# Keeping the residual transposed on chip, and streaming 256 tokens past stationary weights, in a two-layer f32 trunk

## The chip, the cores and the metric

The kernel runs on one core of one Trainium2 chip. The time is the device time of one execution in microseconds (us). Of each kernel the median of several executions is taken; one further execution is profiled, and all rows of a trace come from that one.

## The reference

The program is the trunk of a small decoder: 256 tokens (two tiles of 128), model width 1024, two layers, everything in float32. Each layer is: half a SwiGLU FFN, a token mixer, half a SwiGLU FFN, each behind an RMS norm of its own. The first mixer is native sparse attention (NSA), the second is FoX, attention with a forget gate over keys and values that one shared projection of x (here "kv") made. Cut to what matters:

```python
def rms_norm(x, g):
    return x * lax.rsqrt(jnp.mean(x * x, axis=-1, keepdims=True) + EPS) * g
def swiglu(h, w_in, w_out):                     # w_in (1024, 2*2816), w_out (2816, 1024)
    a, b = jnp.split(h @ w_in, 2, axis=-1)
    return (jax.nn.silu(a) * b) @ w_out
for l in range(2):
    if l == 1: k_sh, v_sh, c_sh = shared_kv(x, kv_norm_g, fox_w_kvf, fox_b_f)
    x = x + 0.5 * swiglu(rms_norm(x, norm_g[l, 0]), ffn_w_in[l, 0], ffn_w_out[l, 0])
    h = rms_norm(x, norm_g[l, 1])
    x = x + (nsa_mixer(h, ...) if l == 0 else fox_mixer(h, ...))   # each ends in o @ w_out, (1024, 1024)
    x = x + 0.5 * swiglu(rms_norm(x, norm_g[l, 2]), ffn_w_in[l, 1], ffn_w_out[l, 1])
return rms_norm(x, final_g)
```

## The kernel before

**Precision.** TensorE multiplies f32r, a rounded f32. Every large product is made in three: each operand is split into a high part and a low part (`thi`, `tlo` of the transposed x; `whi`, `wlo` of the weights; `ghi`, `glo` of the hidden tile), and `three` issues high*high, high*low and low*high into one PSUM bank (lines 396 to 398). ScalarE makes high parts (`hi`, lines 858 and 864), VectorE (DVE) low parts (`lo`, lines 1214 and 1220).

**Weights.** They stream from HBM in 166 units of 1 MB, 128 x 2048 f32 each, through a ring of three buffers, in the order in which TensorE wants them. SyncE asks for unit u as soon as the low part of unit u-3 is made; ScalarE overwrites a slot of `whi` when TensorE has used the unit that was in it (semaphore `unit_used`).

**An FFN.** The hidden width 2816 is cut into 11 chunks of 256 columns (of a and of b). A round of the loop (`ffn`) makes the in-product of one chunk (two units, 48 matmuls) and the out-product of the chunk before (one unit, 24 matmuls). The stationary operand is a 128 x 128 piece of tokens, 512 columns of weights stream past it, and the hidden chunk comes out with tokens on the partitions: `inb[t]` holds 256 columns of a and 256 of b of token tile t. ScalarE applies Silu with the row's 1/rms as its scale (`rstd`, one number a partition), VectorE multiplies by b, TensorE turns the result with four transposes (`hidden_turn`, line 487) so that it can be stationary in the out-product, and the two engines split it. The out-product adds up in the four banks `acc` over all 11 chunks; since the order of the writes differs, four bf16 matmuls with zeros open the banks first (line 501).

**Between stages.** The residual is `xs`, with tokens on partitions. At the end of a stage VectorE adds the banks to it one token tile at a time (`ffn_add`, `mixer_add`), ScalarE sums the squares of a row in one instruction, and TensorE turns x (`turn`, line 390), eight transposes a token tile, which `thi` and `tlo` are then split from with the norm's gain. The turning of tile 0 and of tile 1 stands among matmuls of the stage that ends and of the one that begins.

**Rest.** GpSimd (POOL) builds the bias tables for NSA in the first 45 us, through 16 transfers of its own, splits one unit a mixer, and adds attention outputs. There is no scheduler: the order on each engine is the order of the code, and semaphores hold the engines to each other.

Of the kernel before, what the change touches and what calls it, by code (L numbers as in the profile page):

```python
# [21 lines left out]
F32 = mybir.dt.float32  # L22
# [51 lines left out]
NORMS = ["ffn0", "nsa", "ffn1", "kv", "fox", "ffn3", "final"]  # L74
ADDS = ["ffn0", "nsa", "ffn1", "ffn2", "fox", "ffn3"]

TILE0 = ["nsa", "kv", "fox"]
ADD_BEFORE = {"nsa": "ffn0", "ffn1": "nsa", "kv": "ffn1", "fox": "ffn2", "ffn3": "fox", "final": "ffn3"}


def added(name, t, half):

    before = ADD_BEFORE[name]
    return 4 * ADDS.index(before) + (2 * t + half if before.startswith("ffn") else 2 * half + t) + 1
# [16 lines left out]
def yoco_trunk(nc, x, norm_g, ffn_w_in, ffn_w_out, nsa_w_in, nsa_cmp_pos, nsa_cmp_w1, nsa_cmp_w2,  # L101
               nsa_w_out, rel_bias, kv_norm_g, fox_w_kvf, fox_b_f, fox_w_q, fox_w_out, final_g, out):
    ctx = ExitStack()
    with ctx:
# [13 lines left out]
        xs = sb("xs", [P, NT, D])  # L118
# [5 lines left out]
        sa = sb("sa", [P, NT, FC])  # L124
        gg = sb("gg", [P, NT, FC])
# [20 lines left out]
        zeros = sb("zeros", [32, P], BF16)  # L146
# [16 lines left out]
        rstd_h = sb("rstd_h", [P, NT, H])  # L163
# [36 lines left out]
        squares_out = work[:, D:2 * D]  # L200
        fexp = work[0:H, 0:SEQ]
# [25 lines left out]
        s_sumsq = sem("sumsq")  # L227
        s_rms = sem("rms")
        s_rstd = sem("rstd_ready")
        s_rstd_h = sem("rstd_by_head")  # L230
        s_tt = sem("turned")
        s_thi = sem("turned_hi")
        s_tlo = sem("turned_lo")
        s_silu = sem("silu_done")
        s_g = sem("hidden_ready")
        s_gt = sem("hidden_turned")
        s_ghi = sem("hidden_hi")
        s_glo = sem("hidden_lo")
        s_in0 = sem("hidden_cols_tile0")
        s_out_bank = sem("ffn_out_bank")  # L240
        s_tile0 = sem("tile0_done")
# [68 lines left out]
        def _(sp):  # L310
# [20 lines left out]
            def ffn(f):  # L331
                b = U_FFN[f]
                for i in range(2):
                    load(b + i, ffn_in(f, 0, i, b + i))
                    if b + i == 0:
                        sp.dma_start(xs[:, 1, :], x[0, P:2 * P, :]).then_inc(s_x[1], 16)
# [9 lines left out]
            def matrix(w, b, chunks):  # L346

                for c, col in enumerate(chunks):
                    for i in range(2):
                        u = b + 2 * c + i  # L350
# [4 lines left out]
            sp.dma_start(xs[:, 0, :], x[0, 0:P, :]).then_inc(s_x[0], 16)  # L355
# [9 lines left out]
            matrix(nsa_w_out[0], U_NSA_OUT, [0, CW])  # L365
# [4 lines left out]
            matrix(fox_w_out[0], U_FOX_OUT, [0, CW])  # L370
            ffn(3)
            for t in range(NT):
                for n, done in enumerate([s_y, s_ya]):
                    cols = slice(n * CW, (n + 1) * CW)
                    sp.wait_ge(done, t + 1)
                    sp.dma_start(out[0, t * P:(t + 1) * P, cols], xn[:, t, cols]).then_inc(s_out, 16)
# [4 lines left out]
        def _(pe):  # L381
            def turn(name, t):

                for e in range(2):
                    if name == "ffn0":
                        pe.wait_ge(s_x[t], 16)
                    elif name != "ffn2":
                        pe.wait_ge(s_xadd, added(name, t, e))
                    for k in range(4):
                        mm = pe.transpose(tbanks[2 * t + e][:, k * P:(k + 1) * P],  # L390
                                          xs[:, t, (4 * e + k) * P:(4 * e + k + 1) * P], ident[:, :])
                    mm.then_inc(s_tt, 1)

# [6 lines left out]
            def rows4(slot, half, t, o, wait_third=None):  # L400

                tok = slice(t * P, (t + 1) * P)
                for k in range(4):
                    if k == 2 and wait_third:
                        pe.wait_ge(*wait_third)
                    kk = 4 * half + k
                    mm = three(o, thi[:, kk, tok], tlo[:, kk, tok], whi[slot][:, k * CW:(k + 1) * CW],
                               wlo[slot][:, k * CW:(k + 1) * CW], kk == 0, kk == KT - 1)
# [1368 lines left out]
```

## Time and profile before

| | |
|---|---|
| median of 3 runs | 1088.58 us (1088.22 to 1090.03) |
| profiled execution | 1091.58 us, of which the trace spans 1089.8 us |
| granted TensorE clock, mean | 0.988 |
| busy: TensorE, its weight loads | 97%, 80% |
| busy: VectorE, ScalarE, GpSimd | 56%, 48%, 8% |
| matmuls | 5067 |
| read from HBM | 180 MB, 167 GB/s over the span |

The page says which engine was busy for how long. A matmul's record is longer than the distance to the next one's start, since matmuls are pipelined; times of single matmuls are therefore read as distances between starts in the timeline.

### The profile page before, as it was taken

To read this page: it belongs to the slowest core of one execution; us is meant where nothing else is said; L and a number is where in the kernel's file an instruction comes from. 1 tells how busy PE (TensorE), PEld (TensorE's weight loads), DVE (VectorE), ACT (ScalarE), POOL (GpSimd) and SP (SyncE) were. 2 spreads that over 40 slices of the span, in tenths; PEclk is the share of its full clock that TensorE was granted. 3 is DMA by queue.
4 is the path that set the end of the run, shared out by engine and by line. 5 is a ranking of instruction groups with operands and counts; after the bars stand their busy time and mean duration, and the time that the engine had idled before them with its cause. 6 is when DMAs were issued, how large, how long until landed. Compare 5 with 4: busy or idle time off the path is not lost.

```text
span 1089.8 us, 14059 instructions
## 1 busy us (share of the span) xinstructions
PE 1060.1 (97%) x5067; PEld 872.4 (80%) x5067; DVE 612.5 (56%) x844; ACT 522.7 (48%) x751; POOL 89.4 (8%) x112
## 2 busy tenths in 40 slices
PE   8799999999899999999999999999998999999997
PEld 6688888888677888888888878888886788888886
DVE  4444545677767464445556775454557656444454
ACT  7334344666446364443356454444355646444434
POOL 6300000000202100000000192000002000000000
PEclk9899999999889999999999999999999999999999
DMA  9765465456500245555554655555545135555541
GB/s 269 216 208 187 159 231 193 155 176 210 193 1 1 64 163 194 187 191 170 196 185 155 231 194 192 175 191 186 181 155 194 38 97 193 192 182 189 190 171 39
DMA packets 128675, 182.40 MB, mean 167 GB/s; under 512 B 5929, under 2 KB 100241, under 8 KB 128513
## 3 DMA queue, kind: packets, MB, share of 16 engines
q1 hardware_dynamic: 127008, 176.18, 49.0%
q0 software_dynamic: 1456, 5.72, 2.0%
q8 instruction: 21, 0.34, 0.1%
q14 instruction: 14, 0.11, 0.0%
q10 hardware_dynamic: 176, 0.05, 0.0%
HBM read 180.34 MB, written 1.59 MB: 167 GB/s over the span
## 4 chain that ended last, share of the span: by engine, by line
PE 91%; DVE 4%; ACT 2%; DMA 2%; issue 1%; SPq 0%; DVEq 0%; ACTq 0%
PE inb L396 16%; PE inb L398 16%; PE inb L397 16%; PE acc L396 11%; PE acc L398 11%; PE acc L397 11%; DMA raw<-in_ffn_w_in 2%; PE tb L487 2%; PE inb L603 2%; PE tb L588 1%; PE acc L574 1%; ACT work L979 1%; DVE nmx L1360 1%; PE inb L600 1%; DVE work L1357 1%; DVE wlo L1214 1%
## 5 line engine op out<-in xcount | busy, mean ns | idle before, releaser
L1220 DVE TENSOR_TENSOR wlo<-raw,whi 128x2048 fp32r<-128x2048 f32 x108 | 248.6, 2302 | 247.4 <-ACT whi L864 247.4
L864 ACT CAST whi<-raw 128x2048 fp32r<-128x2048 f32 x108 | 206.5, 1912 | 238.6 <-PE acc L398 117.1
L396 PE MATMUL inb<-whi,thi 128*128 128x512 f32 x784 | 308.1, 393 | 2.0 <-DVE wlo L1214 2.0
L398 PE MATMUL inb<-whi,tlo 128*128 128x512 f32 x784 | 306.1, 390 | 0.0
L397 PE MATMUL inb<-wlo,thi 128*128 128x512 f32 x784 | 306.0, 390 | 0.0
L396 PEld LDWEIGHTS inb<-whi,thi 128*128 128x128 f32 x784 | 147.9, 189 | 32.8 <-issue 2.6
L398 PEld LDWEIGHTS inb<-whi,tlo 128*128 128x128 f32 x784 | 147.7, 188 | 31.3
L397 PEld LDWEIGHTS inb<-wlo,thi 128*128 128x128 f32 x784 | 147.9, 189 | 30.5
L1214 DVE TENSOR_TENSOR wlo<-raw,whi 128x2048 fp32r<-128x2048 f32 x55 | 129.1, 2353 | 46.9 <-ACT whi L858 46.6
L396 PE MATMUL acc<-whi,ghi 128*128 128x512 f32 x320 | 129.0, 403 | 0.0
L398 PE MATMUL acc<-whi,glo 128*128 128x512 f32 x320 | 125.6, 392 | 0.0
L397 PE MATMUL acc<-wlo,ghi 128*128 128x512 f32 x320 | 125.3, 391 | 0.0
L858 ACT CAST whi<-raw 128x2048 fp32r<-128x2048 f32 x55 | 105.2, 1920 | 11.9 <-PE acc L398 9.5
L917 ACT ACTIVATE sa<-inb,rstd 128x256 f32<-128x256 f32 x88 | 37.9, 472 | 145.9 <-PE inb L398 145.8
L1267 DVE SCALAR_TENSOR_TENSOR gg<-inb,rstd,sa 128x256 f32<-128x256 f32 x88 | 39.3, 480 | 73.3 <-ACT sa L917 73.3
L398 PEld LDWEIGHTS acc<-whi,glo 128*128 128x128 f32 x320 | 60.4, 189 | 12.9
L397 PEld LDWEIGHTS acc<-wlo,ghi 128*128 128x128 f32 x320 | 60.5, 189 | 11.2
L396 PEld LDWEIGHTS acc<-whi,ghi 128*128 128x128 f32 x320 | 60.4, 189 | 11.1
L396 PE MATMUL acc<-whi,thi 128*128 128x512 f32 x160 | 63.8, 399 | 0.0
L398 PE MATMUL acc<-whi,tlo 128*128 128x512 f32 x160 | 62.5, 391 | 0.0
L397 PE MATMUL acc<-wlo,thi 128*128 128x512 f32 x160 | 62.4, 390 | 0.0
L979 ACT ACTIVATE work<-work,nmx 128x128 f32<-128x128 f32 (+1 forms) x96 | 42.5, 444 | 14.7 <-DVE nmx L1360 14.6
(235 smaller groups left out, 1008.3 us busy)
## 6 DMA issues: line engine op xcount, KB each, us to landing
raw<-in_ffn_w_in SPq DMA_DIRECT2D x176, 512.0 KB, 4.7
raw<-in_ffn_w_out SPq DMA_DIRECT2D x88, 512.0 KB, 4.0
raw<-in_nsa_w_in SPq DMA_DIRECT2D x20, 512.0 KB, 4.2
raw<-in_fox_w_kvf SPq DMA_DIRECT2D x16, 512.0 KB, 4.5
raw<-in_nsa_cmp_w SPq DMA_DIRECT2D x8, 512.0 KB, 4.4
raw<-in_nsa_w_out SPq DMA_DIRECT2D x8, 512.0 KB, 4.4
raw<-in_fox_w_q SPq DMA_DIRECT2D x8, 512.0 KB, 4.4
raw<-in_fox_w_out SPq DMA_DIRECT2D x8, 512.0 KB, 4.5
```

What stands on the lines that cost most here:

```text
L396: pe.matmul(o, lh, rh, start=start, stop=False, skip_group_check=True)
L397: pe.matmul(o, lh, rl, start=False, stop=False, skip_group_check=True)
L398: return pe.matmul(o, ll, rh, start=False, stop=stop, skip_group_check=True)
L487: mm = pe.transpose(tb[0][:, k * SEQ + t * P:k * SEQ + (t + 1) * P], gg[:, t, k * P:(k + 1) * P], ident[:, :])
L603: mm = pe.matmul(o[:, P + h * DH:P + (h + 1) * DH], pT[:, n % 2, h, (1 + k) * P:(2 + k) * P], v(k, h), start=k == 0, stop=k == 1)
L858: act.copy(whi[u % RING][:, :], raw[u % RING][:, :]).then_inc(s_hi, 1)
L864: act.copy(whi[u % RING][:, :], raw[u % RING][:, :]).then_inc(s_hi, 1)
L917: act.activation(sa[:, t, :], inb[t][:, 0:FC], ACT.Silu, scale=rstd[:, t:t + 1]).then_inc(s_silu, 1)
L979: act.activation(probs[:, n % 2, c0:c0 + w], probs[:, n % 2, c0:c0 + w], ACT.Exp, bias=nmx[:, n % 4, i:i + 1], accum_out=lsum[:, n % 4, i: ...
L1214: dve.tensor_tensor(wlo[u % RING][:, :], raw[u % RING][:, :], whi[u % RING][:, :].bitcast(F32), ALU.subtract).then_inc(s_lo, 1)
L1220: dve.tensor_tensor(wlo[u % RING][:, :], raw[u % RING][:, :], whi[u % RING][:, :].bitcast(F32), ALU.subtract).then_inc(s_lo, 1)
L1267: dve.scalar_tensor_tensor(out=gg[:, t, :], in0=inb[t][:, FC:2 * FC], scalar=rstd[:, t:t + 1], in1=sa[:, t, :], op0=ALU.mult, op1=ALU.mult ...
```

## The change

`xs` goes; `xT` holds the residual transposed, with the 1024 features on the partitions (8 blocks `k` of 128) and 256 tokens along the free axis. Products whose result is wanted transposed now hold 128 x 128 pieces of the weights stationary and stream all 256 tokens:

- the in-products of all FFNs (`hidden_cols`): a and b of a chunk come out with hidden columns on partitions, a in one bank and b in another, so that nothing has to be turned for the out-product;
- the out-products of FFN 0 to 2 (`out_unit`) and both mixers' out-projections (`out_mixer`): the result is a piece of `xT`, two blocks a bank.

The products of the projections (NSA in, kv, FoX q) stay as they are, and so does the out-product of FFN 3, whose result leaves in token rows (`out_natural`); there x is turned back by 16 transposes (`x_turn`).

Since a token is now a column, 1/rms must be known along the free axis: ScalarE squares x, GpSimd adds the eight blocks (`sum_squares`), TensorE multiplies the sum by ones (`spread`), which puts the sum for every token on every partition, ScalarE takes the root into `rB` (128 x 256), and VectorE inverts it (`root`). VectorE multiplies a and b by `rB` on their way out of the banks, and ScalarE takes Silu of the scaled a. In the first chunk of an FFN the products go to the banks `tb`, in all others to `inb`.

The order of units in the mixers' out-projection changes: both column halves for the first half of the rows, then both for the second. The four zeroing matmuls go.

```diff
-            def rows4(slot, half, t, o, wait_third=None):
-                tok = slice(t * P, (t + 1) * P)
-                for k in range(4):
...
-                    mm = three(o, thi[:, kk, tok], tlo[:, kk, tok], whi[slot][:, k * CW:(k + 1) * CW],
-                               wlo[slot][:, k * CW:(k + 1) * CW], kk == 0, kk == KT - 1)
+            def spread(name, bank):
+                pe.wait_ge(s_ssum, NORMS.index(name) + 1)
+                for t in range(NT):
+                    c0 = SEQ + 2 * t
+                    pe.matmul(bank[:, c0:c0 + 2], ssum[:, t * P:(t + 1) * P], ones[:, 0:2], start=True, stop=True)
+                pe.matmul(bank[:, 0:SEQ], ones[:, 0:1].broadcast_to([P, P]), ssum, start=True, stop=True).then_inc(s_rmm, 1)
+            def hidden_cols(slot, k, kk, banks):
+                for m in range(4):
+                    col = slice(k * CW + m * P, k * CW + (m + 1) * P)
+                    o = banks[m // 2][:, (m % 2) * SEQ:(m % 2 + 1) * SEQ]
+                    wh, wl, xh, xl = whi[slot][:, col], wlo[slot][:, col], thi[:, kk, :], tlo[:, kk, :]
+                    pe.matmul(o, wh, xh, start=kk == 0 and m % 2 == 0, stop=False, skip_group_check=True)
+                    pe.matmul(o, wh, xl, start=False, stop=False, skip_group_check=True)
+                    mm = pe.matmul(o, wl, xh, start=False, stop=kk == KT - 1, skip_group_check=True)
+                return mm
+            def out_unit(slot, first, last):
+                h_hi, h_lo = (ghi_last, glo_last) if last else (ghi, glo)
+                for d in range(KT):
+                    for k in range(2):
+                        col = slice(k * D + d * P, k * D + (d + 1) * P)
+                        mm = out_rows(acc_half(d), (whi[slot][:, col], wlo[slot][:, col]), h_hi[:, k, :],
+                                      h_lo[:, k, :], first and k == 0 and d % 2 == 0, last and k == 1)
+                    if last and d in (1, 3, 5):
+                        mm.then_inc(s_bank, 1)
+                return mm
...
-                with pe.Fori(1, NJ - 1) as j:
-                    for half in range(2):
-                        u = b + 2 + half
-                        unit_in(u % RING, half, inb, 3 * (j - 1) + u + 1)
...
-                    out_part(slot, 1, 0)
-                    hidden_turn(2 * j + 2 * n0 + 2)
-                    out_part(slot, 1, 1).then_inc(s_used, 1)
+                chunk_in(1)
...
+                chunk_out(1, True)
+                with pe.Fori(2, NJ - 1) as j:
+                    pe.wait_ge(s_br, j + n0)
+                    chunk_in(j)
+                    chunk_out(j)
...
+            def root(name):
                 dve.wait_ge(s_rms, NORMS.index(name) + 1)
-                step(dve.reciprocal(rstd[:, :], ss[:, NT:2 * NT]))
+                dve.reciprocal(rB[:, :], rB[:, :])
+                step(dve.reciprocal(rstd[:, :], ss[:, 0:NT]))
...
+            def hidden(n, banks, first=False):
...
+                dve.tensor_tensor(sa[:, :, :], banks[0][:, :].rearrange("p (k n) -> p k n", k=2), r_both,
+                                  ALU.mult).then_inc(s_ar, 1)
+                dve.tensor_tensor(gg[:, :, :], banks[1][:, :].rearrange("p (k n) -> p k n", k=2), r_both,
+                                  ALU.mult).then_inc(s_br, 1)
+                dve.wait_ge(s_br, n)
+                dve.wait_ge(s_silu, n)
+                dve.tensor_tensor(gg[:, :, :], sa[:, :, :], gg[:, :, :], ALU.mult).then_inc(s_g, 1)
...
+            def sum_squares(name):
+                for b in range(4):
+                    pool.wait_ge(s_sq, normed_at(name, b))
+                    if b == 0:
+                        step(pool.tensor_tensor(ssum, sq[:, 0, :], sq[:, 1, :], ALU.add))
+                        continue
+                    step(pool.tensor_tensor(ssum_part, sq[:, 2 * b, :], sq[:, 2 * b + 1, :], ALU.add))
+                    both = pool.tensor_tensor(ssum, ssum, ssum_part, ALU.add)
...
+            sum_squares("ffn0")
             small = [(gate_w[:, :, :], nsa_w_in[0, :, D + 6 * KVD:].rearrange("(k p) n -> p k n", p=P)),
...
-            sp.dma_start(xs[:, 0, :], x[0, 0:P, :]).then_inc(s_x[0], 16)
+            for t in range(NT):
+                sp.dma_start(xn[:, t, :], x[0, t * P:(t + 1) * P, :]).then_inc(s_x[t], 16)
```

How the instructions of an engine stand. On TensorE, the end of a round of the FFN loop before, in FFN 0 (tb holds the turned hidden tile gg, acc the out-product, inb the in-product):

```order
L398 MATMUL acc<-whi,glo 128x512
L484 ISA
L487 MATMUL tb<-ident,gg 128x128 [waits hidden_ready]
L487 MATMUL tb<-ident,gg 128x128 x3
L396 MATMUL acc<-whi,ghi 128x512
L397 MATMUL acc<-wlo,ghi 128x512
L398 MATMUL acc<-whi,glo 128x512
```

and the same place now, where the out-product passes into the next round's in-product:

```order
L458 MATMUL acc<-ghi,wlo 128x256
L554 REGISTER_ALU
L554 COMPARE_AND_BRANCH
L448 MATMUL inb<-thi,whi 128x256 [waits unit_lo,hidden_b_scaled]
L449 MATMUL inb<-tlo,whi 128x256
L450 MATMUL inb<-thi,wlo 128x256
```

The transposes and their wait are gone, the streamed operand is 256 wide, and a wait stands at the start of the in-product, for VectorE's reading of the banks.

On VectorE, between the last unit of FFN 0 and the first of NSA, before (xs is the residual, tlo the low part of the turned x):

```order
L1316 SCALAR_TENSOR_TENSOR xs<-acc,xs 128x512 [waits ffn_out_bank]
L1316 SCALAR_TENSOR_TENSOR xs<-acc,xs 128x512 [waits unit_used]
L1214 TENSOR_TENSOR wlo<-raw,whi 128x2048 [waits unit_hi]
L1237 SCALAR_TENSOR_TENSOR tlo<-acc,gains,thi 128x128 [waits turned_hi]
L1237 SCALAR_TENSOR_TENSOR tlo<-acc,gains,thi 128x128 x3
L1237 SCALAR_TENSOR_TENSOR tlo<-acc,gains,thi 128x128 [waits turned_hi]
L1237 SCALAR_TENSOR_TENSOR tlo<-acc,gains,thi 128x128 x3
L1214 TENSOR_TENSOR wlo<-raw,whi 128x2048 [waits unit_hi]
L1226 RECIPROCAL rstd<-ss 128x2 [waits rms]
```

and now:

```order
L1302 SCALAR_TENSOR_TENSOR xT<-acc,xT 128x512 [waits unit_used]
L1311 SCALAR_TENSOR_TENSOR tlo<-xT,gains,thi 128x256 [waits x_hi]
L1311 SCALAR_TENSOR_TENSOR tlo<-xT,gains,thi 128x256
L1311 SCALAR_TENSOR_TENSOR tlo<-xT,gains,thi 128x256 [waits x_hi]
L1311 SCALAR_TENSOR_TENSOR tlo<-xT,gains,thi 128x256
L1265 TENSOR_TENSOR wlo<-raw,whi 128x2048 [waits unit_hi] x2
L1497 TENSOR_TENSOR glo<-gate_w,ghi 128x384 [waits small_split]
L1265 TENSOR_TENSOR wlo<-raw,whi 128x2048 [waits unit_hi]
L1277 RECIPROCAL rB<-rB 128x256 [waits rms]
```

The adds and splits go by feature blocks of all tokens, the second weight unit's lower half (the first of the x2) stands behind all four splits, and the reciprocal of the spread row behind three units.

## Rows read from the trace of the kernel before

**Rows 1.** The page: busy time of the engines; DMA queue of the instructions.

```profile
PE 1060.1 (97%) x5067; PEld 872.4 (80%) x5067; DVE 612.5 (56%) x844; ACT 522.7 (48%) x751; POOL 89.4 (8%) x112
...
q8 instruction: 21, 0.34, 0.1%
```

**Rows 2.** TensorE's waits: engine, line waited for: us, times, longest.

```profile
PE tb L588 <- ACT work L979: 11.6, 5, 5.3
PE tb L487 <- DVE gg L1267: 5.6, 1, 5.6
```

**Rows 3.** Timeline of TensorE in an FFN round: start, length, what, form, count.

```profile
100.63 0.60 PE L487 MATMUL tb<-ident,gg 128*128 128x128 f32 x4
...
102.46 0.39 PE L396 MATMUL inb<-whi,thi 128*128 128x512 f32 x1
...
104.28 0.39 PE L398 MATMUL inb<-whi,tlo 128*128 128x512 f32 x1
...
117.43 0.60 PE L487 MATMUL tb<-ident,gg 128*128 128x128 f32 x4
117.78 0.48 PE L396 MATMUL acc<-whi,ghi 128*128 128x512 f32 x1
118.10 0.40 PE L397 MATMUL acc<-wlo,ghi 128*128 128x512 f32 x1
```

**Rows 4.** The same: 256 columns streamed past 48 stationary ones.

```profile
234.24 0.28 PE L397 MATMUL acc<-tlo,ghi 128*48 128x256 f32 x1
...
236.76 0.28 PE L398 MATMUL acc<-thi,glo 128*48 128x256 f32 x1
```

**Rows 5.** Timeline: weight loads (PEld), small and plain f32 matmuls.

```profile
102.47 0.19 PEld L397 LDWEIGHTS inb<-wlo,thi 128*128 128x128 f32 x1
...
348.81 0.53 PEld L603 LDWEIGHTS inb<-nat,work 128*128 128x128 f32 x4
348.87 0.61 PE L603 MATMUL inb<-nat,work 128*128 128x64 f32 x4
...
353.66 1.02 PE L574 MATMUL acc<-kblk,qT 128*128 128x512 f32 x2
354.52 0.38 PE L576 MATMUL acc<-kblk,qT 128*128 128x256 f32 x1
```

**Rows 6.** Timeline of TensorE: turning x for a norm; the zeroing matmuls.

```profile
204.69 1.03 PE L390 MATMUL tb<-ident,xs 128*128 128x128 f32 x8
205.48 0.48 PE L396 MATMUL acc<-whi,ghi 128*128 128x512 f32 x1
...
396.98 1.03 PE L501 MATMUL acc<-zeros 32*128 32x512 bf16 x4
398.13 0.66 PE L487 MATMUL tb<-ident,gg 128*128 128x128 f32 x4
```

**Rows 7.** The chain from 20 to 55 us, and busy time from 40 to 60.

```profile
30.33 11.83 DMA raw<-in_ffn_w_in
...
51.00 0.43 PE inb L396
...
40.00:60.00 20.00, 14.35 (x54) 11.44 (x53) 8.62 (x7) 8.83 (x7) 2.75 (x3) 0.83 0.78 252
```

**Rows 8.** Groups by form: what, count, busy us, mean ns, idle before.

```profile
L1214 DVE TENSOR_TENSOR wlo<-raw,whi 128x2048 fp32r<-128x2048 f32 x55 | 129.1, 2353 | 46.9 <-ACT whi L858 46.6
...
L1316 DVE SCALAR_TENSOR_TENSOR xs<-acc,xs 128x512 f32<-128x512 f32 x16 | 11.0, 688 | 5.7 <-PE acc L398 5.7
...
L1580 DVE RECIPROCAL work<-work 16x256 f32<-16x256 f32 x1 | 1.7, 1743 | 0.0
...
L878 ACT ACT_TABLE_LOAD x6 | 7.7, 1283 | 0.1
...
L1734 POOL TENSOR_TENSOR xn<-xn,gg 128x256 f32<-128x256 f32 x8 | 5.8, 729 | 18.9 <-DVE gg L1383 18.9
```

**Rows 9.** Timeline: the last matmul.

```profile
1083.60 0.39 PE L398 MATMUL acc<-whi,flo 128*128 128x512 f32 x1
```

More of the change, by code:

```diff
@@ L414, in unit_in @@
                 for t in range(NT):
-                    mm = rows4(slot, half, t, banks[t][:, :])
+                    for k in range(4):
+                        mm = rows(slot, k, 4 * half + k, t, banks[t][:, :])
                 mm.then_inc(s_used, 1)
@@ L895, in turned @@
-            def turned(name, t):
-                for e in range(2):
-                    turned_half(name, t, e)
             def o_hi(g, first):
@@ L941, in ffn, with x_natural, chunk @@
+            def x_natural(t):
+                for e in range(2):
+                    act.wait_ge(s_xnt, 2 * t + e + 1)
+                    act.copy(xn[:, t, e * CW:(e + 1) * CW], tb[e][:, :]).then_inc(s_xnat, 1)
+            def ffn(f):
+                b, n0, name = U_FFN[f], NJ * f, f"ffn{f}"
                 hi(b + 3)
+                if f != 2:
+                    rms(name, inb[0])
+                silu(n0 + 1)
                 hi(b + 4)
[L943 to L945 removed]
+                hidden_hi(n0 + 1, ghi)
+                def chunk(j):
@@ L1004, in _ @@
             act.wait_ge(s_setup, 1)
-            turned_half("ffn0", 0, 0)
+            for b in range(4):
+                x_hi("ffn0", b)
             act.wait_ge(s_raw[0], 32)
@@ L1240, in turned_half @@
                 ins.then_inc(s_tlo, 1)
-            def turned(name, t):
-                for e in range(2):
-                    turned_half(name, t, e)
             def o_lo(g, first):
@@ L1299, in ffn @@
-                last = 2 * n0 + 2 * (NJ - 1)
-                hidden_tile(last, 0)
-                hidden_last_lo(h0 + NJ, 0)
+                chunk(1)
+                with dve.Fori(2, NJ - 1) as j:
+                    chunk(j)
                 lo(b + FFN_UNITS - 1)
-                hidden_tile(last + 1, 1)
+                dve.wait_ge(s_used, 3 * (NJ - 2) + b + 4)
+                hidden(n0 + NJ, inb)
+                hidden_lo(n0 + NJ, glo_last, ghi_last)
                 lo(b + FFN_UNITS)
-                ffn_add(f, 0)
@@ L1399, in _ @@
             dve.wait_ge(s_setup, 1)
-            turned_half("ffn0", 0, 0)
+            x_update("ffn0", 0)
+            for b in range(1, 4):
+                x_update("ffn0", b)
+                x_lo("ffn0", b - 1)
+            x_lo("ffn0", 3)
             dve.wait_ge(s_half0, 1)
```

674 lines of the change are left out of this document (356 added, 318 removed).

## The prediction

> **What bounds the kernel now.** Read the page first: TensorE is busy 97% of the span [rows 1]. No other engine comes near, so the question is how many matmuls TensorE issues, at which step, and where it waits. The table of its waits says that it hardly waits: 11.6 us for softmax work inside the attention, which the change does not touch, and 5.6 us once, for the hidden columns, in the first FFN [rows 2]. The timeline of one FFN round shows the rest [rows 3]. A round starts every 16.80 us (100.63 to 117.43). It holds 72 matmuls of 512 columns and four transposes. Matmuls are pipelined, so a record's length (0.39) is not its cost; the cost is the distance between starts: eight steps from 102.46 to 104.28 are 1.82 us, 0.2275 us each, and 72 of 0.2267 make 16.32. The remaining 0.48 us is the turning of the hidden tile: 0.35 us from 117.43 to 117.78, and a step of 0.32 in place of 0.23 behind it.
>
> **The change, part by part.** The sum is made against the profiled execution, 1,089.8 us of span (1,091.6 with what lies around it); the median of the runs, 1,088.6, is 3 us below that, and I take the difference over as it is.
>
> *The streamed size, the term that decides.* All FFN-in products (4 FFNs x 11 chunks x 48 matmuls), the FFN-out products of three FFNs (3 x 11 x 24) and both mixer out-projections (2 x 48) are converted: 2,112 + 792 + 192 = 3,096 matmuls of 512 columns become 6,192 of 256 columns. Columns streamed stay the same, weight loads double. What counts is the step of a 256-column matmul with a 128-column load. The trace has no such matmul, but both halves of it. With a 48-column stationary operand 256 columns step at 0.1145 us (22 steps from 234.24 to 236.76) [rows 4]; that is half of the 512-column step, 0.1134, plus 1 ns. With a load of 128 columns and next to nothing to stream (64 columns) the step is 0.112: the load records of four such matmuls last 0.53, less 0.19 for one, over three steps, 0.113, and their matmul records 0.61 less 0.275 the same [rows 5]. So a load takes about 0.112 by itself, and the stream about 0.1134. In the FFN the load of the next matmul starts 0.01 us after the start of the running one (102.46 and 102.47) [rows 3, 5], so the two run side by side, and the step should be the greater of them plus a little for the handing over. Lower bound 0.1134. Upper bound: the 512-column step is 0.0134 above the 0.2133 that 512 columns take at 2.4 GHz; if those 13 ns belong to every load and not to the columns, 256 columns step at 0.1067 + 0.0134 = 0.120. The row with the small load stands at 0.1145 and not at 0.120, which speaks for the columns, so I take 0.115. Against the 0.1134 of before that is 1.6 ns x 5,808 (the 384 in the first rounds lie in a stretch that waits for DMA anyway) = +9.3 us. Bounds: 0 and +40.
>
> A rule of the Trainium skill speaks against this: "TensorE: Matmul & The Clock Gate", Part 3 on packing small matmuls, has weight loads overlap running matmuls only where the row groups differ. By it load and stream would add up, some 0.22 us a matmul, and the kernel would be 600 us slower. The trace does not agree: with full row groups the load starts 0.01 us behind the matmul before it, and the 512-column step leaves no room for 0.11 us of load.
>
> *Removed from TensorE.* The turning of the hidden tile: 34 rounds behind the first 60 us x 0.48 = 16.3, three first chunks x 0.5, four last chunks of two half turnings x 0.22: 19.6 us. The zeroing matmuls: 1.15 us a FFN (396.98 to 398.13) [rows 6], three that count: 3.5. The turning of x for a norm: eight transposes take 0.79 (204.69 to 205.48) and 0.08 behind them [rows 6]; 12 groups after the first FFN: 10.5, and 0.8 more in one that ran at half the clock: 11.3. The four small matmuls that spread rstd: 0.6. Together -35.0 us.
>
> *Added to TensorE.* For each of six norms a spread of the sums of squares: a plain f32 matmul of 256 columns (the 512-column one takes 0.86 for its two records, 353.66 to 354.52, so 0.43) and two of 2 columns, two records each at the load's 0.112: 0.88, with the switch 0.95; five count: +4.8. In the last FFN 16 transposes of x back to token rows at 0.11 and two switches: +1.9.
>
> *The boundaries.* Before, x was finished one token tile at a time under matmuls. Now it is finished bank by bank under the last output unit, in steps of 12 x 0.115 = 1.4 us. DVE needs per bank an add (0.69 [rows 8]) and a split of about 0.85, 1.55 us, so it ends some 3 us after TensorE's last matmul; the next product begins with the banks that are ready and wants the last at 4 to 5 us. Behind the splits DVE makes the lower half of the second weight unit (2.3 us): ready at about 5.3, wanted at 5.4. No cover is left there: three boundaries x 0 to 2 us, I take +1. rstd comes later, since GpSimd adds the squares (0.73 for 256 columns, two an x bank), ScalarE loads the table of the root (1.28) and DVE's reciprocal of the spread row takes 1.74 [rows 8]. It is wanted only by the scaling behind the first chunk, which no longer holds TensorE: chunk 0 goes to the two turning banks and chunk 1 streams in 11 us meanwhile. Cost nothing; without that cover, 2 us a norm. In the round VectorE now does three operations of 512 columns in place of two of 256, but it sits in a round of 16.6 us and is wanted a whole product later: nothing.
>
> *The start.* Before, the weights of the second round were asked for at about 30, fell on the 16 transfers of the bias table and took 11.83 us; TensorE ran out and was idle for 5.65 of the 20 us from 40 to 60, and came back at half the clock, 0.43 a step, when the round began at 51.00 (granted clock 0.83 in the mean of the stretch) [rows 7]. Some 7.5 us were lost: the 5.65, and about ten steps that took 0.2 more. Now GpSimd first adds squares, so the bias transfers go out some 13 us later, when the ring of weights is full; on the other side x comes whole ahead of the weights and is turned and split before the first lower half, which by my estimate makes the first matmul 5 us later, and the next request for weights too. I take a gain of 5 us of the 7.5; range -8 to +3.
>
> *The tail.* The last matmul starts at 1083.60, 6.2 us before the end [rows 9]. The two token tiles of the last output now finish within the last 5.5 us and not one of them early, and the first tile's chain holds a table load (1.28): DVE comes to the second tile later. +2.3 us.
>
> Sum: 9.3 - 35.0 + 4.8 + 1.9 + 1.0 - 5.0 + 2.3 = -20.7 us; 1,088.6 - 20.7 = 1,068 us. A tie is at a step of 0.1186 (0.115 + 20.7/5,808).
>
> **The rivals.**
> 1. The load does not hide (slower). Place: the FFN round. If loading 128 columns and streaming 256 take turns on something, or each load costs its 13 ns, the step is 0.120 to 0.122. For it: stream 0.1134 and load 0.112 are nearly equal, while 512 columns left the loader free half of the time, so this kernel never tried it. Against it: the 48-column row. Time at 0.120: +38.3 in place of 9.3, so 1,097; at 0.122, 1,109. It decides from 0.1186 on.
> 2. Boundaries bite. Nothing of the start's gain and 2 to 3 us lost at each of six norms, since updates, splits, squares and the root stand in one line on DVE and ScalarE that nothing but the first chunk covers. For it: the margin of 0.1 us above. Against: only one unit is that close. +5 and +14: 1,087.
> 3. The code no longer fits its fetching. A round is now 288 instructions of TensorE (144 loads, 144 matmuls) and before 152. Queue q8 brought instructions 21 times in 0.34 MB, 16 KB a time [rows 1], so a round spans more than one piece. If each jump back fetched one again, at about 1 us, 28 jumps cost 28 us or more: 1,096. Against: of 5,067 matmuls and as many loads 32 rounds of 76 are repeats; the 5,270 instructions left, against 0.34 MB, are 64 bytes each, a plausible size, so the rounds of before seem not to have been fetched again.
>
> "Advanced Engine Details and Errata", section ISA Cache, of the Trainium skill gives TensorE 128 KB for code, in lines of 256 instructions; by that rival 3 fails. No row here shows the size.
>
> **How the numbers follow.** Forecast, step below 0.1186 and boundaries as said: 0.70, with its own range 1,055 to 1,084. Rival 1: 0.18. Rival 2: 0.08. Rival 3: 0.04. The likeliest gives 1,068. At the low end the step is 0.1134 (-9) and the start gives 8 (-3): 1,056; so 1,055. At the high end rival 1 at 0.120 is taken in: 1,098; what lies above is about one in ten. Two in a thousand, 2 us, is what a measurement tells. Faster: the forecast nearly whole and most of rival 2: 0.74; same 0.05; slower 0.21.
>
> **What would show it.** In the new trace: a distance of 0.115 between starts in an FFN round, rounds of 16.56 us (144 x 0.115) and no transposes in them; the second round starting by about 46 us, not 51.0; no wait of TensorE for weights' lower halves or x's at a norm over 1 us; the root ready before TensorE has finished chunk 0; a tail of about 8 us. A step near 0.120 with rounds of 17.3 us would make it wrong, and with it the sign; so would a pause of a microsecond at each jump back.

## The result, and the profile after

The changed kernel takes 1,110.7 us in the median of four runs (1,108.3 to 1,113.2); the kernel before takes 1,089.3 in the four runs beside it (1,088.2 to 1,092.8). The ratio is 1.0191, with a 95% interval of 1.0158 to 1.0224: slower by 21 us, where 20.7 us of gain were forecast. The profiled execution of the changed kernel has a span of 1,111.2 us, 21.4 us more than the one before; it is the slowest of its four. One execution of repaired_late, a run further down, took 1,548.4 us at a mean granted clock of 0.63 and is left out of that run's time.

The page of the changed kernel, busy time of the engines and the queue of the instructions:

```profile
PE 1074.2 (97%) x7923; PEld 1016.6 (91%) x7923; DVE 685.7 (62%) x836; ACT 510.9 (46%) x657; POOL 124.8 (11%) x154
...
q8 instruction: 32, 0.52, 0.2%
```

TensorE is busy for 97% as before, with 2,856 more matmuls, and the loader of the weights is now busy for 91% of the span and not for 80% [rows 1]. Instructions were brought 32 times, 0.52 MB, against 21 times and 0.34 MB. That is 11 more, and the loops jump back 28 times, so the code has grown and was not fetched again at each jump.

TensorE's timeline at three boundaries of one FFN round (start, length, instruction, form):

```profile
422.49 0.28 PE L448 MATMUL inb<-thi,whi 128*128 128x256 f32 x1
...
433.89 0.28 PE L450 MATMUL inb<-thi,wlo 128*128 128x256 f32 x1
434.01 0.28 PE L456 MATMUL acc<-ghi,whi 128*128 128x256 f32 x1
...
439.77 0.28 PE L448 MATMUL inb<-thi,whi 128*128 128x256 f32 x1
```

From 422.49 to 434.01 stand 96 in-products, from 434.01 to 439.77 stand 48 out-products: 0.120 us each in both (6,056 of the 6,192 converted matmuls start 0.118 to 0.122 us ahead of the next). The round is 17.28 us without a transpose in it; before it was 16.80 with four [rows 3]. The turning has gone as said, and more than its price has come back in the step.

TensorE's waits in the changed kernel (line waited for: us in total, times, longest):

```profile
PE tb L617 <- ACT work L1026: 11.2, 5, 5.3
PE tb L448 <- DVE wlo L1482: 4.0, 1, 4.0
PE inb L398 <- DVE wlo L1265: 4.0, 2, 2.0
PE acc L398 <- DVE wlo L1265: 2.0, 1, 2.0
PE inb L663 <- POOL xn L1827: 1.9, 1, 1.9
```

The first is the softmax work of before [rows 2]. The second is the start: TensorE waits for x and the first lower half. The next two are new: at the three norms nsa, kv and fox it waits 2.0 us each for the lower half of the second weight unit. The last is new too: ahead of the first out-projection TensorE waits for the last columns of o, the attention's output. The nsa norm, TensorE and VectorE, shows what is late:

```profile
214.50 0.39 PE L400 MATMUL inb<-whi,tlo 128*128 128x512 f32 x1
216.87 0.50 PE L398 MATMUL inb<-whi,thi 128*128 128x512 f32 x1 [1.97 <-DVE wlo L1265]
...
218.42 0.63 PE L400 MATMUL inb<-whi,tlo 128*128 128x512 f32 x1
218.84 0.63 PE L398 MATMUL inb<-whi,thi 128*128 128x512 f32 x1
```

```profile
208.52 0.68 DVE L1302 SCALAR_TENSOR_TENSOR xT<-acc,xT 128x512 f32<-128x512 f32 x1
...
210.75 0.68 DVE L1302 SCALAR_TENSOR_TENSOR xT<-acc,xT 128x512 f32<-128x512 f32 x1
211.36 2.71 DVE L1311 SCALAR_TENSOR_TENSOR tlo<-xT,gains,thi 128x256 fp32r<-128x256 f32 x4
213.99 5.03 DVE L1265 TENSOR_TENSOR wlo<-raw,whi 128x2048 fp32r<-128x2048 f32 x2
```

VectorE makes all splits of x first and begins the weights' lower half at 213.99, when TensorE has 0.7 us of products left. From 208.52 to 210.75 it is busy without a gap with one bank, an add and two splits: 2.23 us. Behind the wait seven matmuls start 0.43 us behind the one before, 0.2 more than the others; with the step ahead of them and the spread behind, the nsa norm takes 1.6 us longer than the kv norm. The granted clock of TensorE in stretches around it (stretch: length, PE busy and count, clock, DMA share, GB/s) says why:

```profile
213.00:218.00 5.00, 3.03 (x14) 0.98 0.02 4
218.00:222.40 4.40, 4.40 (x16) 0.64 1.02 348
222.40:227.00 4.60, 4.60 (x22) 1.00 1.00 336
588.00:592.00 4.00, 2.02 (x9) 1.00 0.00 0
```

A matmul of 512 columns at 0.43 is one at 1.2 GHz. The kv norm has the same wait of 2.0 us (in the stretch from 588) and no slow step behind it.

The clock falls at a second new place, behind the wait for o:

```profile
372.59 1.09 PE L663 MATMUL inb<-ident,xn 128*128 128x128 f32 x4 [1.89 <-POOL xn L1827]
...
374.12 0.42 PE L456 MATMUL acc<-thi,whi 128*128 128x256 f32 x1
374.33 0.41 PE L457 MATMUL acc<-tlo,whi 128*128 128x256 f32 x1
...
378.43 0.28 PE L456 MATMUL acc<-thi,whi 128*128 128x256 f32 x1
```

From 372.59 to 378.43 are 5.84 us. In the run lo_early below, which has the same wait there and keeps the clock, the same instructions take 3.34 (368.97 to 372.31). So 2.5 us are lost behind this wait. At 1.2 GHz a matmul of 256 columns steps at 0.213 and one of 512 at 0.427, which is the time of their columns alone: the 13 ns that both pay beyond their columns at 2.4 GHz do not show there.

The start and the end (the same view from 0 to 80, then the timeline's last rows of TensorE and VectorE):

```profile
0.00:20.00 20.00, 12.49 (x62) 0.83 0.60 193
20.00:40.00 20.00, 20.00 (x168) 1.00 0.91 274
40.00:60.00 20.00, 20.00 (x169) 1.00 0.95 262
60.00:80.00 20.00, 19.15 (x160) 1.00 0.63 217
```

```profile
1103.23 0.40 PE L400 MATMUL acc<-whi,flo 128*128 128x512 f32 x1
...
1107.63 0.49 DVE L1718 TENSOR_SCALAR qT<-qT,rstd 128x512 f32<-128x512 f32 x1
```

The granted clock from 0 to 20 is 0.83, and 1.00 before: TensorE waits 4.0 us for its first product and then steps at 0.213 until 19.7. The 5.65 us of idle TensorE between 40 and 60 [rows 7] are gone. What is left of them is 0.85 us between 60 and 80. The last matmul starts 8.0 us before the end, 6.2 before [rows 9].

### The profile page after: what moved, and what is told of

It is laid out like the page before. It is cut to its first block, busy times and chain, and to the rows that moved or that the text cites. A ratio compares the mean times of both kernels' runs of the same rounds, so it can differ in the third digit from the quotient of the medians.

```text
span 1111.2 us, 19709 instructions
## 1 busy us (share of the span) xinstructions
PE 1074.2 (97%) x7923; PEld 1016.6 (91%) x7923; DVE 685.7 (62%) x836; ACT 510.9 (46%) x657; POOL 124.8 (11%) x154
## 4 chain that ended last, share of the span: by engine, by line
PE 89%; DVE 6%; ACT 2%; DMA 2%; issue 1%; SPq 0%; POOL 0%; DVEq 0%; ACTq 0%
PE inb L448 13%; PE inb L449 13%; PE inb L450 13%; PE acc L456 7%; PE acc L458 7%; PE acc L457 7%; PE acc L398 4%; PE acc L400 4%; PE acc L399 4%; DVE tlo L1311 2%; PE inb L632 2%; PE tb L617 2%; PE tb L448 1%; PE tb L449 1%; PE tb L450 1%; PE acc L603 1%
## 5 line engine op out<-in xcount | busy, mean ns | idle before, releaser
L448 PE MATMUL inb<-thi,whi 128*128 128x256 f32 x1280 | 362.4, 283 | 0.8 <-DVE gg L1353 0.8
L449 PE MATMUL inb<-tlo,whi 128*128 128x256 f32 x1280 | 362.4, 283 | 0.0
L450 PE MATMUL inb<-thi,wlo 128*128 128x256 f32 x1280 | 362.4, 283 | 0.0
L448 PEld LDWEIGHTS inb<-thi,whi 128*128 128x128 f32 x1280 | 245.8, 192 | 1.4 <-issue 1.0
L449 PEld LDWEIGHTS inb<-tlo,whi 128*128 128x128 f32 x1280 | 245.8, 192 | 0.4
L450 PEld LDWEIGHTS inb<-thi,wlo 128*128 128x128 f32 x1280 | 245.8, 192 | 0.0
L457 PE MATMUL acc<-glo,whi 128*128 128x256 f32 x480 | 135.9, 283 | 0.0
L456 PE MATMUL acc<-ghi,whi 128*128 128x256 f32 x480 | 135.9, 283 | 0.0
L458 PE MATMUL acc<-ghi,wlo 128*128 128x256 f32 x480 | 135.9, 283 | 0.0
L458 PEld LDWEIGHTS acc<-ghi,wlo 128*128 128x128 f32 x480 | 92.2, 192 | 0.0
L1361 DVE TENSOR_TENSOR glo<-gg,ghi 128x512 fp32r<-128x512 f32 x40 | 29.8, 746 | 26.6 <-ACT ghi L968 26.6
```

The lines of the kernel that those rows point to most:

```text
L448: pe.matmul(o, wh, xh, start=kk == 0 and m % 2 == 0, stop=False, skip_group_check=True)
L449: pe.matmul(o, wh, xl, start=False, stop=False, skip_group_check=True)
L450: mm = pe.matmul(o, wl, xh, start=False, stop=kk == KT - 1, skip_group_check=True)
L456: pe.matmul(o, wh, h_hi, start=start, stop=False, skip_group_check=True)
L457: pe.matmul(o, wh, h_lo, start=False, stop=False, skip_group_check=True)
L458: return pe.matmul(o, wl, h_hi, start=False, stop=stop, skip_group_check=True)
```

## Experiments

Two theories stood against each other after this reading. The first: the step of 0.120 is what a matmul of 256 columns with 128 loaded costs, whatever stands around it, and it carries the loss. The second: the step is a feature of this kernel (its layout or the work of the other engines), or the loss sits in the new waits.

**The steps by themselves** (bench). The changed kernel, with a stretch in the second FFN in which TensorE alone works:

```diff
+            def bench():
+                tl = tlo[:, :, :].rearrange("p k n -> p (k n)")
+                for load, stream in [(128, 512), (128, 384), (128, 320), (128, 288), (128, 256), (128, 224),
+                                     (128, 192), (128, 128), (96, 256), (64, 256), (32, 256), (64, 512)]:
+                    for i in range(24):
+                        pe.matmul(acc[i % 4][0:load, 0:stream], thi[:, i % KT, 0:load],
+                                  tl[:, 0:stream], start=True, stop=True)
+                for i in range(24):
+                    pe.matmul(acc[0][:, 0:SEQ], thi[:, 0, 0:P], tl[:, 0:SEQ], start=True, stop=True)
```

> The changed kernel with a stretch of 312 extra matmuls in the second FFN, ahead of its second round, with the other engines idle: products of the x tiles with the x tiles into the four output banks, which the FFN overwrites, 24 for each pair of columns loaded and columns streamed. Theory A (every matmul pays 13 ns that do not depend on its columns): step = columns / 2.4 GHz + 13 ns, so 512: 0.227, 384: 0.173, 320: 0.147, 288: 0.133, 256: 0.120, 224: 0.112 (load-bound), 192 and 128: 0.112; with 96, 64 or 32 columns loaded and 256 streamed still 0.120. Theory B (the 13 ns of 512 columns grow with the columns, and 0.120 comes from load and stream of nearly equal length): 384: 0.170, 320: 0.142, 288: 0.128, and 256 falls from 0.120 with 128 columns loaded to 0.114 with 64 or 32. Theory C (0.120 comes from what the other engines do in an FFN round): 256 columns step below 0.118 in this quiet stretch.

Measured, as the median distance between the starts of neighbouring records of one shape, in ns:

```
columns streamed    512  384  320  288  256  224  192  128
128 loaded          227  173  147  133  120  111  111  111
 96 / 64 / 32, 256 streamed:  117 / 113 / 113;   64 loaded, 512 streamed: 229
```

The last group of 24, all with one stationary operand and one bank, can be read straight off the timeline:

```profile
442.56 3.05 PE L506 MATMUL acc<-tlo,thi 128*128 128x256 f32 x24
445.44 0.28 PE L448 MATMUL inb<-thi,whi 128*128 128x256 f32 x1
```

From 442.56 to 445.44 are 24 steps of 0.120. With 128 columns loaded every figure is theory A's, within 1 ns: columns at 2.4 GHz and 13 ns, and never below the load's 0.111. Theory C (under 0.118 with the other engines idle) falls, and so does theory B for 128 columns loaded (0.128 at 288; 0.133 measured). The small loads are not as A has them: 256 columns step at 0.113 with 64 or 32 loaded, and theory B had 0.114.

**The small loads** (bench2, bench3). The same stretch with other lists of shapes, 32 matmuls each:

```diff
-                for load, stream in [(128, 512), (128, 384), ...
+                for load, stream in [(128, 256), (112, 256), (96, 256), (80, 256), (64, 256), (48, 256),
+                                     (128, 512), (96, 512), (64, 512), (32, 512), (64, 384)]:
-                    for i in range(24):
+                    for i in range(32):
```

> As bench, 32 matmuls each, to see on what the fixed part depends: 256 columns streamed with 128, 112, 96, 80, 64 and 48 loaded; 512 with 128, 96, 64 and 32; 384 with 64. Theory A (fixed part set by the columns loaded: 13 ns at 128, 11 at 96, 7 at 64 or fewer): 512 with 64 or 32 loaded step at 0.220. Rival (the fixed part belongs to the matmul, and small outputs only let short streams run closer): 0.227 or more, as the one row of bench with 64 loaded and 512 streamed says.

```
256 streamed, loaded 128 112  96  80  64  48        512 streamed, loaded 128  96  64  32     384, loaded 64
                     120 113 116 113 113 113                             227 229 229 231              174
```

The fixed part does not shrink with the load: at 512 columns it is 13 to 18 ns for every load. Of these three sizes only 256 gains from fewer loaded columns, 7 ns. bench3 went around that size, with this list and nothing else changed:

```diff
+                for load, stream in [(64, 320), (64, 288), (64, 272), (64, 256), (64, 240), (64, 224), (64, 192),
+                                     (64, 128), (112, 320), (112, 288), (112, 240), (128, 272), (128, 264),
+                                     (128, 248), (128, 240)]:
```

> As bench, 32 matmuls each, around the size at which 128 columns loaded cost more than fewer: 64 loaded with 320, 288, 272, 256, 240, 224, 192 and 128 streamed; 112 loaded with 320, 288 and 240; 128 loaded with 272, 264, 248 and 240. Theory A (columns / 2.4 GHz + 13 ns at any load, and the 0.113 of 256 columns with small loads is an exception of that one size): 64 loaded: 320: 0.147, 288: 0.133, 272: 0.127, 240: 0.113, 224: 0.107, 192: 0.093; 128 loaded: 272: 0.127, 264: 0.123, 248: 0.117, 240: 0.113. Theory D (with short streams the matmul's fixed part is only 7 ns, and 128 columns of load add 7 where load and stream are nearly equal): 64 loaded: 240: 0.107, 224: 0.100; 112 loaded with 240: 0.107; and somewhere between 256 and 288 the small loads change over to 13 ns.

```
streamed         320  288  272  264  256  248  240  224  192  128
 64 loaded       145  132  125       113       107  103   89   60
112 loaded       147  132                      110
128 loaded                 125  120       113  112
```

Neither theory is whole. Theory D's 0.107 at 240 with 64 loaded and the change to the longer fixed part between 256 and 272 are there, its 0.100 at 224 (0.103 measured) and its 0.107 with 112 loaded (0.110) are not. With 128 loaded the sizes just around 256 lie up to 4 ns below theory A. The figures are medians; single steps of a group lie up to some 10 ns around them. What stands is the table: 256 columns step at 0.113 with 48, 64, 80 or 112 loaded and at 0.120 with 128. With 64 loaded the part beyond the columns is 7 to 10 ns from 128 to 256 columns streamed and 12 to 16 ns from 272 on. Why that is so was not settled.

**The size alone, in the kernel before** (halves). Every 512-column matmul of the 36 looped FFN rounds becomes two of 256 with the same stationary columns:

```diff
+                if halved[0]:
+                    a, b = slice(0, 256), slice(256, 512)
+                    pe.matmul(o[:, a], lh, rh[:, a], start=start, stop=False, skip_group_check=True)
+                    pe.matmul(o[:, b], lh, rh[:, b], start=False, stop=False, skip_group_check=True)
...
```

> The kernel before, in whose 36 looped FFN rounds each matmul of 512 columns is two of 256 with the same stationary columns: 2,592 become 5,184, and nothing else differs. Step 0.120 (theories A, B): 2,592 x (0.240 - 0.2267) = +34.5 us, 1,123. Step 0.115, as the prediction had it: +8.6 us, 1,097. If the step of the changed kernel has to do with its own layout or its wait pattern and not with the size, also 1,097.

Measured: 1,122.1 us, ratio 1.0286 (1.0250 to 1.0322), which is +31 us (27 to 35). Its timeline, the first in-product of two neighbouring rounds and the end of one with the matmul behind it:

```profile
107.97 0.28 PE L400 MATMUL inb<-whi,thi 128*128 128x256 f32 x1
...
125.56 0.28 PE L405 MATMUL acc<-whi,glo 128*128 128x256 f32 x1
125.68 0.28 PE L400 MATMUL inb<-whi,thi 128*128 128x256 f32 x1
```

The round is 17.71 us, 0.91 more than before [rows 3]: 144 x 0.120 = 17.28, and the turning. The price of the smaller size shows in the old layout and with the old order of the engines, and near the 34.5 us that the first theory gives.

**The turning** (turns). The kernel before, with one transpose of the hidden tile in place of four in the looped rounds (three quarters of the turned hidden columns are left out, so the output is not the trunk's):

```diff
-                for k in range(2):
+                for k in range(parts):
...
-                    hidden_turn(2 * j + 2 * n0 + 2)
+                    hidden_turn(2 * j + 2 * n0 + 2, [0], 1)
```

> The kernel before, with three of the four transposes of the hidden tile left out in the 36 looped FFN rounds (so the hidden columns of those rounds are partly stale). It prices the term of the sum that was taken from the change: three transposes of 0.11 us and what the switch between kinds of matmul costs. If the 0.48 us of a round are the four transposes' own time, -0.33 x 36 = -12 us, 1,077. If a fixed switch is most of it, -5 us or less. If the turning were free in truth, no change.

Measured: 1,078.4, ratio 0.9883 (0.9850 to 0.9916), -13 us (-16 to -9). The timeline (first in-products of neighbouring rounds are 16.46 apart, 0.34 less than before; the row of the one transpose):

```profile
119.84 0.39 PE L396 MATMUL inb<-whi,thi 128*128 128x512 f32 x1
...
134.81 0.27 PE L487 MATMUL tb<-ident,gg 128*128 128x128 f32 x1
134.84 0.48 PE L396 MATMUL acc<-whi,ghi 128*128 128x512 f32 x1
...
136.30 0.39 PE L396 MATMUL inb<-whi,thi 128*128 128x512 f32 x1
```

So the term for the turning of the hidden tile was right: three transposes fewer save 0.34 us a round, 0.11 us each.

**The waits** (lo_early, repaired, repaired_late). In lo_early only VectorE's order at three norms is changed:

```diff
                     for b in range(1, 4):
                         x_update(name, b)
+                        if b == 3:
+                            lo(u + 1)
                         x_lo(name, b - 1)
                     x_lo(name, 3)
-                    lo(u + 1)
```

> The changed kernel with the split of the second weight unit's lower half made ahead of the last two splits of x at the three norms that are not mixed with an output projection's (nsa, kv, fox). Theory (those three waits of 2.1 us are VectorE's order, and the half clock behind the first is their consequence): waits fall to about 0.3 each and the ten slow steps go, -7 us against the changed kernel, 1,104. Rival (VectorE's work as a whole is too long there, so the wait only moves to the last split of x): within 2 us of the changed kernel.

Measured: 1,107.5, ratio 1.0171 (1.0145 to 1.0198); its interval overlaps the changed kernel's, so the times alone don't tell it. The waits and the clock do:

```profile
PE inb L398 <- DVE tlo L1311: 1.4, 2, 0.7
...
PE acc L398 <- DVE tlo L1311: 0.7, 1, 0.7
```

```profile
216.00:220.00 4.00, 4.00 (x22) 1.00 0.53 184
```

The three waits are 0.7 us each in place of 2.0, now for x's split, and the clock stays whole behind the nsa norm: 3.9 us of waits and 1.6 us of slow steps, 5.5 in all, of the 7 expected. The medians differ by 3.2 us and the profiled spans by 8.3. In part that is the clock behind the two waits for o: here it is whole behind the one in NSA (2.5 us less) and falls behind the one in FoX, 0.9 us long, where it costs 1.4 us (the twelfth product behind it starts 3.17 us after the transposes and not 1.77). Whether the clock falls behind such a wait thus differs between two traces, and one trace a kernel does not say how often it does. A part of the rival is in it: 0.7 us of each wait is VectorE's work as a whole. In repaired the first out-projection unit is also split again, half of it behind the attention's last values:

```diff
             def project_first(b, first):
-                out_mixer(b, first, 0, 0)
+                out_mixer(b, first, 0, 0, range(0, 2))
             def project_out(b, first):
+                out_mixer(b, first, 0, 0, range(2, 4))
                 turn_o(3, first)
```

> The changed kernel with two waits mended: the second unit's lower half split early (as in lo_early), and the second half of the first out-projection unit put back behind the attention's last work, ahead of the turning of the last columns of o. Theory (what makes the change slower is the step of 0.120, and the waits are a smaller part): the two waits for xn (2.05 and 1.05 us) go, so 3 us below lo_early, 1,104, still 15 us above the kernel before. Rival (the waits and what they set off are the larger part): at or below the kernel before, 1,089.

Measured: 1,100.9, ratio 1.0085 (1.0052 to 1.0118), so 9 us above the kernel before (6 to 13). Both waits for xn (the tile of o) at the turning of o are gone from the table of waits; the profiled span is 2.6 us under lo_early's. The medians differ by 6.6, more than the traces account for (3.1 us of waits and 1.4 of slow steps), and the kernels before beside the two differ by 2.6 themselves. With the waits mended the kernel is still slower than before. The last of the three holds the bias transfers back as well:

```diff
             pool.wait_ge(s_setup, 2)
+            pool.wait_ge(s_used, 8)
```

> The repaired form of the changed kernel, with the bias transfers held back until eight weight units are used, as in late. In the changed kernel they fell on the third round's weights, for which ScalarE stood 10 us and TensorE 1 us. Theory: 1 to 2 us below repaired, 1,099, and still above the kernel before. Rival (the start is worth as much here as in late): -4 us, 1,097.

Measured: 1,099.9, ratio 1.0073 (1.0040 to 1.0106): no difference from repaired that a measurement can tell. Its trace has no wait between 50 and 80 us.

**The kernel before, improved** (late, best). The same line in the kernel before:

> The kernel before, with GpSimd's transfers of the bias table held back until eight weight units are used. Theory (the second round's weights were late because they fell on the 16 bias transfers): the 5.65 us wait and the ten steps at half the clock go, -7 us, 1,082. Rival (the weights are late because they are asked for late, whatever else is on the queues): within 2 us of before.

Measured: 1,084.3, ratio 0.9956 (0.9940 to 0.9971). The stretch from 40 to 60 us, which had 5.65 us idle and a clock of 0.83 [rows 7]:

```profile
40.00:60.00 20.00, 20.00 (x94) 1.00 0.47 160
```

ScalarE's first split of the second round's weights, in the kernel before and in late:

```profile
42.26 1.90 ACT L864 CAST whi<-raw 128x2048 fp32r<-128x2048 f32 x1 [12.71 <-DMA raw<-in_ffn_w_in]
```

```profile
35.50 1.91 ACT L864 CAST whi<-raw 128x2048 fp32r<-128x2048 f32 x1 [5.78 <-DMA raw<-in_ffn_w_in]
```

These weights are asked for at 29.76 in the one and at 29.93 in the other, and are there 6.8 us earlier in late. The line holds back all of GpSimd's work on the bias, but while the weights are under way (29.8 to 42.2) that work consists of the 16 transfers. The cause of the wait is thus shown: these transfers, and not the time at which the weights were asked for. Of the 7 us expected 4.8 came by the ratio; the two profiled executions differ by 10.2 (1,079.6 against 1,089.8), and executions of one kernel by some 5 us. In best, on top of it, the zeroing matmuls are left out and the first product of each bank starts it, and the first chunk's hidden tile is turned behind the next products:

```diff
-                for a in acc:
-                    pe.matmul(a[:, :], zeros[:, :], zeros[:, :].unsqueeze(1).broadcast_to([32, 4, P]),
-                              start=True, stop=False, skip_group_check=True)
...
+                pe.wait_ge(s_lo, b + 3)
+                for t in range(NT):
+                    pe.wait_ge(s_g, 2 * n0 + t + 1)
+                    mm = rows4((b + 2) % RING, 0, t, inb[t][:, :])
+                mm.then_inc(s_used, 1)
                 hidden_turn(2 * (n0 + 1))
...
+                unit_in((b + 3) % RING, 1, inb, b + 4)
+                round_out(1, True)
+                with pe.Fori(2, NJ - 1) as j:
```

> The kernel before, with the bias transfers held back (as in late), without the zeroing matmuls (the first output product of each bank starts it) and with the first chunk's hidden tile turned behind the first half of the second round's products, where its wait is covered. Theory: 1.15 us of zeroing and 0.27 of wait in each of four FFNs, so 5 us below late, 1,079, and faster than both kernels. Rival: ScalarE and VectorE take the hidden tile later and their splits of the third round's weights slip, so no more than late, 1,084.

Measured: 1,077.3, ratio 0.9894 (0.9866 to 0.9922): by the ratio 11.6 us under the kernel before, and faster than both kernels. Its page:

```profile
PE 1049.2 (98%) x5051; PEld 866.1 (81%) x5051; DVE 612.9 (57%) x844; ACT 522.5 (49%) x751; POOL 88.6 (8%) x112
```

It keeps the 512-column products. TensorE has 16 matmuls fewer and is busy for 98%; the profiled span is 4.9 us under late's. The two changes that best adds to late were not measured apart.

## Why the prediction was wrong

The forecast was -20.7 us and the traces differ by +21.4. Against each step:

- **The streamed size, the step that failed.** The prediction had "the step should be the greater of them plus a little for the handing over", took 0.115, and wrote +9.3 us. The step is 0.120, the upper bound that it named: (0.120 - 0.1134) x 5,808 = +38.3. That is 29 of the 42 us of error. The 13 ns over the columns' own time were held to belong to the columns, because of the row with 48 stationary columns [rows 4]. At full clock and with 128 columns loaded they are paid once a matmul, whatever it streams (halves shows it in the old kernel): 512, 384, 320, 288 and 256 streamed all carry them (bench). With fewer columns loaded a matmul of 256 columns or less carries only 7 to 10 ns (0.113 at 256 and 0.107 at 240 with 64 loaded), and so the nearest row was near in the streamed columns and far in what mattered, the load. It was rival 1, and of its two wordings "each load costs its 13 ns" is the one that fits; that load and stream take turns does not, since the load lies beside the stream down to 0.111. The tie stood at 0.1186, so by the forecast's own sum 0.120 turns the sign.
- **The boundaries.** "Three boundaries x 0 to 2 us, I take +1": they cost 3 x 2.1 us of distance between starts, and 1.6 us of slow steps behind the first, 8.0 together and 7.0 more than taken. The working put the lower half at 5.3 us and the want at 5.4; in the trace it is ready 2.1 us after it is wanted. The working had VectorE done with x 3 us after TensorE's last output product; the trace has it done at 213.99, 4.7 us after the norm's first product started (209.26), and the lower half behind that. The term that was too small is VectorE's work for a bank: 1.55 us in the working, which had 0.85 for the split; in the trace it is 2.23, of which the split, two instructions of 256 columns, takes 1.6. lo_early shows that the order of the work was the larger part of the wait (2.0 us down to 0.7). This is rival 2's mechanism at three of its six norms; that the clock would fall behind such a wait stood in neither.
- **A wait that the sum did not have.** The first out-projection unit no longer stands partly behind the attention, and TensorE waits for o: 2.05 and 1.05 us. Behind the first the clock fell and took 2.5 us more. repaired takes both waits away, and its trace has the clock whole at both places.
- **The start.** -5.0 was taken. The second round's products start at 46.98, before at 50.80; the third round's at 65.27, before at 68.86, which with one slower step behind it leaves a gain of 3.5 for all that lies ahead. First products start 5 us later (15.2 against 10.2), as estimated, some 20 of them step at half the clock, and the bias transfers now fall on the third round's weights.
- **The tail.** +2.3 taken, +1.8 measured (8.0 against 6.2).
- **Removed and added.** The rounds hold no transposes and turns prices three of them at 0.34 us a round; the zeroing matmuls are gone. The spread takes 0.9 us a norm, as taken. No row speaks against the 35.0 and the 6.7, but the turning of x (11.3 of the 35.0) was priced by no run. The "2 x 48" for the out-projections should read 2 x 96; the sum used the right 192.
- **Rival 3.** Instructions were fetched 32 times in all and the step at a jump back is 0.120 as elsewhere: nothing is paid there.

By these numbers: 38.3 - 35.0 + 6.7 + 8.0 + 3.1 + 2.5 - 3.5 + 1.8 = +21.9 us, against 21.4 between the profiled spans. Without the mendable parts (three waits of 2.1 down to 0.9, the slow steps at both places, the 3.1) it is +10.9, against 10.5 between the profiled spans of repaired and before, and 9 by its ratio. So the change would lose with these waits covered whole too, by an estimate from the same terms: the step takes 38 us and the additions 7, and the turnings, the zeroing and the rest give 35.

## What to carry to other kernels

Halving the columns that a matmul streams is not free even where its load is hidden: here, at full clock, a matmul of 512 or of 256 columns with 128 loaded cost 13 ns beyond its columns, and 3,096 matmuls more ate all that the saved transposes gave. When a sum hangs on 5 ns of a step that no row shows, measure that step by itself first (24 matmuls in a quiet place are enough), and don't read it off a row that agrees in one operand only. Price an engine's work by the instructions that it will run: VectorE needed 2.23 us a bank at the boundaries and not the 1.55 taken, and there was no room for that. Look first for what is idle now: the one line that keeps the bias transfers off the weights and the removal of the zeroing gave 11.6 us in the old layout.

## What the runs showed of the hardware that was not expected

- f32r matmuls with 128 columns loaded step at columns / 2.4 GHz + 13 ns (227, 173, 147, 133, 120 ns for 512, 384, 320, 288, 256; 10 to 12 ns at 272, 264 and 248) and not under 111 ns; with 64 loaded 128 columns step at 60.
- With 256 columns streamed the step is 113 ns for 48, 64, 80 and 112 columns loaded, 116 for 96 and 120 for 128. At 512 fewer loaded columns gain nothing (229 to 231 ns). The mechanism was not found.
- At a granted clock of 0.5 (1.2 GHz) f32r matmuls of 256 and 512 columns with 128 loaded step at 0.213 and 0.427 us, their columns alone. The 13 ns show only at 2.4 GHz.
- Three waits of 2.0 us at like places: behind one the granted clock was 0.64 for 4.4 us, behind the one at 588 it stayed at 1.00. With the wait at 0.7 it stayed at 1.00 at the first too. Behind the wait of 1.9 us for o the clock fell in the changed kernel and not in lo_early, and behind the one of 0.9 us in FoX it fell in lo_early and not in the changed kernel: the same wait in the same place may cost 2.5 us more or nothing.
